# An encoder layer on eight cores: attention with queries on partitions, gates computed first, units interleaved into the next group's projections

## The reference, cut to what matters

```python
h = rms_norm(x, norm_pre)                      # 8192 x 4096
p = h @ w_in                                   # columns: q|k|v|attn_gate|conv_B|conv_C|conv_x|conv_gate|merge_A|merge_B
q, k = partial_rotary(q, cos, sin), partial_rotary(k, cos, sin)   # first 32 of 128 dims: halves t1, t2
# 32 query heads, 8 key heads; blocks of 128 queries see 384 keys, |i-j| <= 128
scores = q @ k.T * scale, -inf outside the band
m = maximum(max(scores), sink);  pr = exp(scores - m)
a = (pr / (sum(pr) + exp(sink - m))) @ v
y_a = (a * silu(attn_gate)) @ w_attn_out
y_b = (conv_B * conv3(conv_C * conv_x) * silu(conv_gate)) @ w_conv_out
m = sigmoid(merge_A + b) * y_a + sigmoid(merge_B + b) * y_b
out = x + rms_norm(m @ w_out, norm_post)
```

## Time and profile before

| | |
|---|---|
| time, median of 3 runs | 5762.01 us (5761.17 to 5766.19) |
| profiled execution, its own time | 5765.06 us |
| its span, core 4 (the slowest) | 5763.5 us |
| spans of the eight cores | 5751.9 to 5763.5 us |
| mean granted TensorE clock of the cores | 0.980 to 0.984 |
| TensorE busy | 5454.5 us, 95% |
| keys and values, all heads | 179.24 to 464.30 us |
| queries, gates, attention | 464.30 to 1673.66 us |

### The profile page before, as it was taken

How to read it: one execution, slowest core, us unless ns; L and a number is a source line. 1 busy time by engine, 2 the same in 40 slices (tenths; PEclk the granted TensorE clock), 3 DMA queues, 4 the chain that set the end, 5 groups by cost and what they waited for, 6 DMA issues and landing times.

```text
span 5763.5 us, 64440 instructions; the slowest of 8 cores (5751.9 to 5763.5 us)
## 1 busy us (share of the span) xinstructions
PE 5454.5 (95%) x28304; PEld 2746.9 (48%) x28304; DVE 766.6 (13%) x938; ACT 761.1 (13%) x1481; POOL 207.6 (4%) x397
## 2 busy tenths in 40 slices
PE   1899999999989999999999999999999999999987
PEld 1454444444444444445555555555554444444433
DVE  3211122122210000001111110111110001111122
ACT  3202333333320000000000000000000000000100
POOL 0000000000000000000000000000000000000000
PEclk8899999999999999999999999999999999999988
DMA  5343333333354444455655656565555556664475
GB/s 178 60 67 64 58 66 66 61 65 66 57 118 101 92 99 92 96 106 88 98 96 92 95 94 97 88 97 97 92 95 103 113 114 153 148 156 165 153 248 183
DMA packets 95924, 601.77 MB, mean 104 GB/s; under 512 B 11616, under 2 KB 11872, under 8 KB 38816
## 3 DMA queue, kind: packets, MB, share of 16 engines
q0 software_dynamic: 53520, 413.16, 42.2%
q1 hardware_dynamic: 42128, 184.49, 9.1%
HBM read 923.45 MB, written 92.27 MB: 176 GB/s over the span
## 4 chain that ended last, share of the span: by engine, by line
PE 90%; ACT 3%; DMA 3%; DVE 2%; issue 1%; SPq 0%; ACTq 0%; POOL 0%; DVEq 0%; POOLq 0%
PE bank L276 80%; PE bank L780 6%; DMA xr<-x_ext 1%; PE bank L528 1%; PE bank L478 1%; DVE hnb L309 1%; PE bank L482 1%; ACT sgt L565 1%; DMA xt<-x_ext 1%; PE bank L460 1%; ACT junk L301 1%; ACT sgt L563 1%; DMA agT<-ag_sp 1%; PE bank L318 0%; PE bank L465 0%
## 5 line engine op out<-in xcount | busy, mean ns | idle before, releaser
L276 PE MATMUL bank<-hT,wr 128*128 128x512 bf16 (+2 forms) x19968 | 3929.8, 356 | 1.0 <-DVE hT L326 1.0
L276 PEld LDWEIGHTS bank<-hT,wr 128*128 128x128 bf16 x19968 | 1948.6, 98 | 1817.3 <-issue 24.0
L780 PE MATMUL bank<-wr,mT 128*128 128x512 bf16 x2048 | 449.6, 383 | 30.3 <-DVE oB L798 26.0
L276 PE MATMUL bank<-agT,wr 128*128 128x512 bf16 x2048 | 450.1, 381 | 8.1 <-DMA agT<-ag_sp 8.1
L276 PE MATMUL bank<-cbT,wr 128*128 128x512 bf16 x2048 | 442.2, 379 | 0.0
L780 PEld LDWEIGHTS bank<-wr,mT 128*128 128x128 bf16 x2048 | 201.4, 98 | 278.4 <-issue 46.5
L276 PEld LDWEIGHTS bank<-agT,wr 128*128 128x128 bf16 x2048 | 200.4, 98 | 252.7 <-issue 13.0
L276 PEld LDWEIGHTS bank<-cbT,wr 128*128 128x128 bf16 x2048 | 200.2, 98 | 241.9
L99 POOL DMA_DIRECT2D wr<-w_in x272 | 144.5, 531 | 4116.2 <-PE bank L276 3944.5
L469 ACT ACTIVATE pT<-bank 128x128 bf16<-128x128 f32 (+2 forms) x384 | 141.7, 378 | 468.1 <-PE bank L465 464.0
L478 PE MATMUL bank<-pT,vtok 128*128 128x128 bf16 (+2 forms) x384 | 106.4, 277 | 88.9 <-DVE agf L499 88.0
(11 more groups left out here) (71 smaller groups left out, 1564.0 us busy)
## 6 DMA issues: line engine op xcount, KB each, us to landing
wr<-w_in POOLq DMA_DIRECT2D x272, 1024.0 KB, 8.8
wr<-wo_bf SPq DMA_DIRECT2D x64, 1024.0 KB, 6.0
wr<-w_a POOLq DMA_DIRECT2D x32, 1024.0 KB, 8.9
wo_bf<-w_o POOLq DMA_DIRECT2D x32, 1024.0 KB, 15.9
wr<-w_b POOLq DMA_DIRECT2D x32, 1024.0 KB, 8.9
xt<-x_ext SPq DMA_DIRECT2D x10, 2048.0 KB, 7.7
ma_sp<-mst SPq DMA_DIRECT2D x32, 512.0 KB, 8.5
gb_sp<-gst SPq DMA_DIRECT2D x32, 512.0 KB, 8.6
```

Of the source, the lines that this page charges most:

```text
L276: e.matmul(o, l, r, start=s, stop=p))
L780: s=(kc == 0), p=(kc == KC - 1): e.matmul(o, l, r, start=s, stop=p))
```

## The change

All that concerns the queries, keys, values and gates is written anew.

- **Gates first.** 32 gate projections run on their own after the norm. ScalarE applies Silu in one instruction for each half, and the result goes to memory (`sg_sp`, f32, 512 KB a head).
- **Groups.** For each of 8 key heads `keys(g)`, `values(g)`, `queries(g)` run in turn. `keys` has two chunks of 512 and one matmul of 256 (both halos) per step. `values` makes the values directly with tokens on partitions: 10 token tiles x 32 steps of 128x128 matmuls, `hT` stationary, no transposes. `queries` has 4 heads.
- **Rotation** (`rotary`) by VectorE straight from PSUM: 4 instructions for each chunk of 512, on 16, 16, 48 and 48 partitions. The columns of q and k are permuted on the host so that the halves lie at partitions 0 and 32.
- **Attention in 128 units**, two heads by one block of 128 queries each. `unit_S`: 2 matmuls of 384 keys with queries on partitions (banks 4 and 5), the mask added to PSUM by VectorE, `reduce_max` over both banks with the sink as a 385th column, a scaling, exp on ScalarE with the negated maximum as bias and the sum accumulated, reciprocal on VectorE, scaling into bf16 on ScalarE. `unit_T`: 6 transposes into bank 6 and one ScalarE copy. `unit_V`: 3 matmuls of 256 queries into bank 7, and one VectorE product with the gate, loaded from `sg_sp`.
- **Interleaving.** `attention()` makes 152 steps; step s does `unit_S(s)`, `unit_T(s-2)`, `unit_V(s-3)`, where 16 of 18 steps of a group hold a unit. `slot()` runs one step at 3 places in each projection (after contraction steps 8, 16 and 24) and after value tiles 3, 6 and 9: 18 slots a group. The attention of group g lies in the projections of group g+1, that of the last group in 10 merge_B projections (`emit_LB`), which are taken from the 32 of stage (6).
- Removed: the ones, `rmat` and identity mask matmuls, the value transposes, the DMA swap of the keys, `esink`.

```diff
+        def rotary(psrc, n, off, tab, dst, waits):
+            nonlocal rot_free
+            v = rt[:, off:off + n]
+            w1 = rsw[:, off:off + n]
+            cs, sn = tab(cosT), tab(sinT)
+            sh = (lambda a: a.rearrange("p (a b) -> p a b", b=128)) if len(psrc.shape) == 3 else (lambda a: a)
+            o1 = cx.op("dve", lambda e: e.tensor_tensor(sh(w1)[0:16], psrc[32:48], sn[32:48], ALU.mult),
+                       waits=fl(waits, rot_free, tc1, tc2))
+            o2 = cx.op("dve", lambda e: e.tensor_tensor(sh(w1)[32:48], psrc[0:16], sn[0:16], ALU.mult),
+                       waits=fl(waits, rot_free))
+            o3 = cx.op("dve", lambda e: e.tensor_tensor(sh(v), psrc[0:48], cs[0:48], ALU.mult),
+                       waits=fl(waits, rot_free))
+            o4 = cx.op("dve", lambda e: e.tensor_tensor(dst, sh(v), sh(w1), ALU.add), waits=[o1, o2, o3])
+            rot_free = o4
+            return o3, o4
...
+        def unit_S(u):
+            g, n, hp = u // 16, (u % 16) // 2, u % 2
+            gb = g % 2
+            if u % 16 == 0:
+                sS[0] = cx.op("dve", lambda e, g=g: e.tensor_copy(
+                    s2[:, :, 385:386], sinks[:, 4 * g:4 * g + 2].rearrange("p (a b) -> p a b", b=1)),
+                    waits=fl(bfree[4], bfree[5], t_sk))
+                sS[1] = cx.op("dve", lambda e, g=g: e.tensor_copy(
+                    s2[:, :, 0:1], sinks[:, 4 * g + 2:4 * g + 4].rearrange("p (a b) -> p a b", b=1)),
+                    waits=fl(bfree[4], bfree[5], t_sk))
+            if n % 4 == 0 and hp == 0:
+                th = n // 4
+                sgl_ready[th] = cx.dma("sp", sgl[th][:], sg_sp[4 * g:4 * g + 4, :, th * 512:(th + 1) * 512]
+                                       .rearrange("h p t -> p h t"), sgs[th], waits=fl(sgl_free[th], sg_spill[-2:], t_rz))
+            for i in range(2):
+                hl = hp * 2 + i
+                ts = cx.op("pe", lambda e, i=i, hl=hl, n=n, gb=gb: e.matmul(
+                    banks[4 + i][:, 1:385], qT[gb][:, hl, n * 128:(n + 1) * 128], kT[gb][:, n * 128:n * 128 + 384],
+                    start=True, stop=True), waits=fl(k_ready[gb], q_ready[gb], bfree[4 + i], sS))
+            if u % 16 == 15:
+                k_free[gb] = ts
+                q_free[gb] = ts
+            mi = 0 if n == 0 else (2 if n == 7 else 1)
+            uc = (u % 4) * 2
+            lo = 1 - hp
+            edges = s2[:, :, 1:385].rearrange("p b (k n) -> p b k n", n=128)[:, :, 0::2, :]
+            m1 = cx.op("dve", lambda e, mi=mi: e.tensor_tensor(
+                edges, edges, masks[:, mi * 512:(mi + 1) * 512].rearrange("p (b k n) -> p b k n", b=2, k=2), ALU.add),
+                waits=[ts])
+            m2 = cx.op("dve", lambda e, lo=lo, uc=uc: e.reduce_max(nm[:, uc:uc + 2], s2[:, :, lo:lo + 385], AX.X, negate=True),
+                       waits=[m1])
+            m3 = cx.op("dve", lambda e, uc=uc: e.tensor_scalar(nm[:, uc:uc + 2], nm[:, uc:uc + 2], SCALE, None, ALU.mult),
+                       waits=[m2])
+            te = []
+            for i in range(2):
+                hl = hp * 2 + i
+                te.append(cx.op("act", lambda e, i=i, hl=hl, uc=uc, lo=lo: e.activation(
+                    pr[hl][:], banks[4 + i][:, lo:lo + 385], AF.Exp, bias=nm[:, uc + i:uc + i + 1], scale=SCALE,
+                    accum_out=den[:, uc + i:uc + i + 1]), waits=fl(m3, pr_free[hl])))
+                bfree[4 + i] = [te[i]]
+            rd = cx.op("dve", lambda e, uc=uc: e.reciprocal(rden[:, uc:uc + 2], den[:, uc:uc + 2]), waits=fl(te))
+            for i in range(2):
+                hl = hp * 2 + i
+                bi = (u % 3) * 2 + i
+                sc = cx.op("act", lambda e, i=i, hl=hl, bi=bi, uc=uc, hp=hp: e.activation(
+                    pb16[bi][:], pr[hl][:, hp:hp + 384], AF.Copy, scale=rden[:, uc + i:uc + i + 1]),
+                    waits=fl(rd, te[i], pb_free[bi]))
+                pr_free[hl] = sc
+            p_ready[u] = sc
+        def unit_T(u):
+            for k in range(3):
+                for i in range(2):
+                    bi = (u % 3) * 2 + i
+                    tt = cx.op("pe", lambda e, k=k, i=i, bi=bi: e.transpose(
+                        bbf[6][:, k * 256 + i * 128:k * 256 + (i + 1) * 128], pb16[bi][:, k * 128:(k + 1) * 128],
+                        identb[:]), waits=fl(p_ready[u], bfree[6]) if k + i == 0 else (), signal=(k == 2 and i == 1))
+            pb_free[(u % 3) * 2] = pb_free[(u % 3) * 2 + 1] = tt
+            ev = cx.op("act", lambda e, b=u % 2: e.activation(pT[b][:], bbf[6][:, 0:768], AF.Copy),
+                       waits=fl(tt, pT_free[u % 2]))
+            bfree[6] = [ev]
+            pT_ready[u] = ev
+        def unit_V(u):
+            g, n, hp = u // 16, (u % 16) // 2, u % 2
+            gb = g % 2
+            c0 = hp * 256
+            for k in range(3):
+                tv = cx.op("pe", lambda e, k=k, n=n, gb=gb, c0=c0, b=u % 2: e.matmul(
+                    banks[7][:, c0:c0 + 256], vtok[gb][:, n + k, :], pT[b][:, k * 256:(k + 1) * 256],
+                    start=(k == 0), stop=(k == 2)),
+                    waits=fl(v_ready[gb], pT_ready[u], bfree[7]) if k == 0 else (), signal=(k == 2))
+            pT_free[u % 2] = tv
+            if u % 16 == 15:
+                v_free[gb] = tv
+            th, nn = n // 4, n % 4
+            av = cx.op("dve", lambda e, hp=hp, th=th, nn=nn, c0=c0: e.tensor_tensor(
+                ago[th][:, hp * 2:hp * 2 + 2, nn * 128:(nn + 1) * 128],
+                banks[7][:, c0:c0 + 256].rearrange("p (a b) -> p a b", b=128),
+                sgl[th][:, hp * 2:hp * 2 + 2, nn * 128:(nn + 1) * 128], ALU.mult),
+                waits=fl(tv, sgl_ready[th], ago_free[th]))
+            bfree[7] = [av]
+            if nn == 3 and hp == 1:
+                sgl_free[th] = av
+                ago_free[th] = cx.dma("sp", ag_sp[4 * g:4 * g + 4, :, th * 512:(th + 1) * 512].rearrange("h p t -> p h t"),
+                                      ago[th][:], ags[th], waits=[av])
+                ag_spill.append(ago_free[th])
...
+        def attention():
+            for s in range(18 * NKVH + 8):
+                for fn, back in ((unit_S, 0), (unit_T, 2), (unit_V, 3)):
+                    g, r = divmod(s - back, 18)
+                    if s >= back and r < 16 and g < NKVH:
+                        fn(g * 16 + r)
+                yield
...
+        def hooked(src, chunks, bks):
+            si, lt = ring.load(src)
+            wt = ring.slots[si][:].rearrange("p (k c) -> p k c", c=128)
+            for kc in range(KC):
+                for ci, ((tok0, n), bi) in enumerate(zip(chunks, bks)):
+                    fn = (lambda e, o=banks[bi][:, 0:n], l=wt[:, kc, :], r=rhs_h(kc, tok0, n), s=(kc == 0), p=(kc == KC - 1):
+                          e.matmul(o, l, r, start=s, stop=p))
+                    t = cx.op("pe", fn, waits=fl(lt, bfree[bi]) if kc == 0 else (),
+                              signal=(kc == KC - 1 and ci == len(chunks) - 1))
+                if kc % 8 == 7 and kc != KC - 1:
+                    slot()
+            ring.free[si] = t
+            return t, wt, si
...
+        def keys(g):
+            gb = g % 2
+            t, wt, si = hooked(w_in[T_K + g], OWN2, (0, 1))
+            hx = hT[:].rearrange("p k (a b) -> p k a b", b=128)
+            for kc in range(KC):
+                th = cx.op("pe", lambda e, kc=kc: e.matmul(
+                    banks[3][:, 0:256].rearrange("p (a b) -> p a b", b=128), wt[:, kc, :], hx[:, kc, 0::9, :],
+                    start=(kc == 0), stop=(kc == KC - 1)), waits=fl(bfree[3]) if kc == 0 else (), signal=(kc == KC - 1))
+            ring.free[si] = th
+            for i in range(2):
+                ea = cx.op("act", lambda e, gb=gb, i=i: e.activation(
+                    kT[gb][:, 128 + i * 512:128 + (i + 1) * 512], banks[i][:], AF.Copy), waits=fl(t, k_free[gb]))
+            for i in range(2):
+                o3, o4 = rotary(banks[i][:], 512, i * 512, lambda tb, i=i: tb[:, 128 + i * 512:128 + (i + 1) * 512],
+                                kT[gb][0:48, 128 + i * 512:128 + (i + 1) * 512], fl(t, ea, k_free[gb]))
+                bfree[i] = [o3, ea]
+            p3 = banks[3][:, 0:256].rearrange("p (a b) -> p a b", b=128)
+            ea = cx.op("act", lambda e, gb=gb: e.activation(halo(kT[gb][:]), p3, AF.Copy), waits=fl(th, k_free[gb]))
+            o3, o4 = rotary(p3, 256, 0, lambda tb: halo(tb[:]), halo(kT[gb][:])[0:48], fl(th, ea, k_free[gb]))
+            bfree[3] = [o3, ea]
+            k_ready[gb] = [o4, ea]
...
+        def values(g):
+            gb = g % 2
+            si, lt = ring.load(w_in[T_V + g])
+            wt = ring.slots[si][:].rearrange("p (k c) -> p k c", c=128)
+            for t in range(10):
+                bi = (2, 3, 2)[t // 4]
+                col = (t % 4) * 128
+                for kc in range(KC):
+                    tv = cx.op("pe", lambda e, bi=bi, col=col, kc=kc, t=t: e.matmul(
```

(90 more changed lines are left out.)

342 lines of the change are left out of this document (70 added, 272 removed).

## The result

The changed kernel took 5830.7 us (median of 4 runs) against 5764.1, a ratio of 1.0119 with a 95% interval of 1.0101 to 1.0137; by the profiled executions' spans 5828.8 - 5763.5 = 65.3 us more. Forecast was 5805 us, 43 more.

The account below looks back on a forecast made before the run. TensorE, busy 95% of the span, was taken to bound the kernel. Work 1291.5 + waits 181 + fillers 19 + clock 41 = 1532.5 against 1494.4, +38; with +5.5 elsewhere +43: 5805 us, range 5745 to 5872.

Parts of the forecast that it names:

- TensorE's own work: Gates, groups and attention units without waits: 1291.5 us, 203 us below the 1494.4 the two stages took before.
- The rival of slow small matmuls: Value matmuls, 320 in a row, take half as much again (0.084 us each): 72 us more, 5877 us; chance 0.06.
- The waits: TensorE waiting on attention chains and rotations: 25.9 us per group, 181 for 7 groups, plus 19 in filler projections.
- The clock: Low TensorE clock after each wait of 4 to 6.6 us, 1.4 us each: 41 us, bounds 16 and 81.
- the rival in which it stays up: TensorE's clock stays up through the waits, costing 16 us or less instead of 41: 5780 us or somewhat below; chance 0.13.
- The rival of a shorter chain: ScalarE's exps and scalings in a unit overlap, 1.2 us shorter, so waits shrink: 5724 us, faster than before; chance 0.17.
- Table loads in the fillers: Sigmoid between Exps in merge_B filler projections: a 1283 ns load in each chain; the skill's drain would add some 14 us.
- The edges: Outside the rebuilt part: larger masks at the start +0.5 us, later read-back of `ag_sp` into `agT` +5 us.

Follow-up runs that it names:

- the mended kernel: Changed kernel with transposes before scores, rotation spread among units by bank deadlines, attention one slot later: 5585.6 us, ratio 0.9701 to the kernel before.

## Why the prediction was right, and which term was off

Taken apart by the two traces, the part from the end of the norm to the first merge_A projection (without 138 us of fillers) took 1561.3 us where 1532.5 was the sum. To split it I add up TensorE's records of this part from each start to the next: what such a matmul takes at full clock is work, what it takes more at low clock is the clock's, the rest is wait.

- **TensorE's own work, 1291.5 us.** Right: 441.75 for the gates, 90.45 for a group without attention, 17.86 for the values. The rival of slow small matmuls is out. Of the Trainium skill's 81 ns for N=128 ("TensorE: Matmul & The Clock Gate", Back-to-back issue gap) nothing was seen: 56 ns over 320 in a row.
- **The waits, 181 + 19 = 200 us forecast.** 201 measured, counted as the forecast counts, from the start that was due; the profile's idle time, which begins at the modelled end of the matmul before, is 185: 98 at the transposes on ScalarE's copy, 53 at the scores on the exps, 33 at the groups' first units, 1 at the values. One by one, as idle time: 1.41 where 1.6 was worked out, 3.53 + 2.10 and some tenths where 6.3 was, 6.32 for 6.6, 4.12 for 4.2, 0.95 for 0.9; from the start that was due the first is 1.56, the last but one 4.28. The rows with no equal were near: the mask add to PSUM took 0.70 (0.69), the reduce_max 0.96 (0.96), scalings 0.61 (0.62), the copy 0.79 (0.81). The two orders that made the waits were shown to be the cause by undoing each, 116 and some 80 us, and both, with the banks' deadlines kept and attention one slot later, 245.
- **The clock, 41 us forecast, range 16 to 81.** This is the term that was mis-sized. What is left after work and waits is 1561.3 - 1291.5 - 201 = 69 us, by the records 68, and the experiment without units gives 395 - 126 - 201 = 68. By the records, where the forecast has 29 waits at 1.4 us each:
  - The 14 pairs behind a rotation (3.53 and 2.10 us with slow scores between) cost 35 us, 1.6 to 3.2 each, 2.5 in the mean; why one costs half of another is open. The forecast took each pair as one wait of 6.3 us at 1.4, which is 20.
  - The 15 single waits of 4.1 to 6.3 us cost 22 us, 1.3 to 1.9 each, near the 21 taken.
  - Four of the five waits at the transposes in the fillers, 1.9 to 3.0 us long, cost 9 us. The forecast had no clock term for them, though the kernel before lost its clock behind 12 of 31 waits of 2.64 us.
  - At its start the part is still at the low clock from the norm, 2 us.

  With the waits behind the rotation gone the clock is 1.00 between 715 and 1400 us, without the rotation and in the mended kernel. So it followed the waits; the rival in which it stays up is out.
- **The rival of a shorter chain** is out: an exp took 0.58 us, a scaling 0.61, the copy 0.79, where 0.58, 0.62 and 0.81 were worked out, and the waits are what they were forecast to be, not 40% less.
- **Table loads in the fillers.** 11 switches, each 1.28 us with the ACTIVATE right behind, as at L612 before; the drain that the Trainium skill puts behind a load ("ScalarE: Activation LUTs", What ACT_TABLE_LOAD costs) is not on the path. ScalarE's timeline in the changed kernel:

```profile
1724.10 1.28 ACT L450 ACT_TABLE_LOAD   x1 [1.51 <-DVE nm L445]
1725.39 0.58 ACT L450 ACTIVATE pr<-ps,nm 128x385 f32<-128x385 f32 x1
```

- **The edges.** The first x tile landed 1.9 us later (0.5 forecast). The read-back, whose fence holds the last `gb_sp` spill too, started 12.1 us into the merge_A projections (10.5 forecast):

```profile
1892.65 29.74 SPq L99 DMA_DIRECT2D agT<-ag_sp  x8
...
1923.05 8.26 PE L275 MATMUL ps<-agT,wr 128*128 128x512 bf16 x24 [7.92 <-DMA agT<-ag_sp]
```

but it cost 2.8 us more than before, not 5. The rest of the program, with the fillers taken from it, was 6.7 us shorter; this lies in the output stage (513.5 us before, 506.9 after), whose code is unchanged, and why was not followed up. Sum: 67.3 + 1.9 + 2.8 - 6.7 = 65.3, the difference of the spans.

The forecast was 22 us low: the clock term 27 us and the waits 1 too small, against the 7 us in the output stage, which nothing in the forecast foresaw and which brought its sum nearer by luck. The bounds that the prediction names for its own forecast, 5750 to 5870, are not what its clock and wait bounds add up to (5744 to 5881); the measured time lies within both.

## What to carry to other kernels

When units are interleaved into another engine's stream, write down each helper engine's list in order and ask what stands ahead of the instruction that the next slot waits for: here two changes of order were worth 116 and some 80 us, and 245 us once the rotation's deadlines were kept too, in a change whose plain work was a gain. Work that nobody waits for soon (a rotation for the next group) belongs where its engine is idle anyway, between an instruction and the answer from the other engine, and its deadline is the release of the bank that it reads. Before rewriting a stage, look for the one wait that recurs: moving one statement of the old kernel gave 1.1%.

## What the runs showed of the hardware

The granted clock's price depends on how the waits lie. 2.64 us of wait alone lowered it in 12 of 31 cases of the kernel before, at 1.3 us each; 28 waits of 1.4 to 1.8 us in the groups of the run without rotation did not once (granted clock 1.00); single waits of 4.1 to 6.3 us did each time, at 1.3 to 1.9 us; two waits of 3.53 and 2.10 us with 1.04 us of slow matmuls between them held it at 0.56 over 10 us and cost 3.1 us, and the 14 such pairs 1.6 to 3.2. 320 matmuls of 128 columns with new weights each started 0.056 us apart. VectorE instructions on 16 partitions took 0.68 us for 512 elements, as long as those on 48, where one on 128 took 0.70.
